# Hybrid decoder layer on one core: gate tables by one fp32r product a token, with the norm, y and routing edits that come with it

## The reference, cut to what matters

```
def peer_ffn(x, w_q, sub_keys, u_tab, v_tab):      # K = 16, 8 heads, 128 keys a side
    s = einsum('nhpd,pkd->nhpk', qry, sub_keys)
    s_top, i_top = top_k(s, K)
    cand = s_top[:, :, 0, :, None] + s_top[:, :, 1, None, :]      # 16 x 16 sums
    best, pos = top_k(cand.reshape(N, H, K * K), K)
    expert = take_along_axis(cand_id, pos)          # i * 128 + j
    gate = softmax(best)
    hid = gelu(einsum('cd,chkd->chk', xc, u_tab[expert]))
    return einsum('chk,chkd->cd', gate * hid, v_tab[expert])
```

## Time and profile before

| | us |
|---|---|
| median of 3 runs (lowest, highest) | 1108.76 (1108.48, 1110.25) |
| profiled execution | 1108.59 |
| its span in the trace | 1106.6 |
| PE busy | 1083.8 (98%) |
| DVE busy | 775.9 (70%) |
| ACT busy | 556.8 (50%) |
| POOL busy | 174.1 (16%) |

### The profile page before, as it was taken

How to read it: one execution, slowest core, us unless ns; L and a number is a source line. 1 busy time by engine, 2 the same in 40 slices (tenths; PEclk the granted TensorE clock), 3 DMA queues, 4 the chain that set the end, 5 groups by cost and what they waited for, 6 DMA issues and landing times.

```text
span 1106.6 us, 19897 instructions
## 1 busy us (share of the span) xinstructions
PE 1083.8 (98%) x6760; PEld 969.9 (88%) x6760; DVE 775.9 (70%) x1399; ACT 556.8 (50%) x903; POOL 174.1 (16%) x112
## 2 busy tenths in 40 slices
PE   9999999999999999999999999999999999999995
PEld 6888887678999999999999999998888888888884
DVE  4457657477999888898997777765555555555556
ACT  4347534554345555554455555554555444555442
POOL 2040002203000022222222545520000000000002
PEclk9999999999999999999999999999999999999998
DMA  7554444344455544445444444446555555555552
GB/s 283 186 191 153 135 170 134 107 160 132 155 171 177 177 164 166 153 157 166 152 134 159 144 139 146 133 152 228 190 192 193 197 195 190 190 194 193 197 194 96
DMA packets 52616, 186.50 MB, mean 169 GB/s; under 512 B 6224, under 2 KB 6608, under 8 KB 52576
## 3 DMA queue, kind: packets, MB, share of 16 engines
q1 hardware_dynamic: 51152, 181.82, 49.1%
q0 software_dynamic: 848, 3.15, 0.7%
q10 hardware_dynamic: 576, 1.05, 0.3%
HBM read 184.94 MB, written 1.05 MB: 168 GB/s over the span
## 4 chain that ended last, share of the span: by engine, by line
PE 73%; issue 12%; DVE 5%; POOL 5%; DMA 3%; ACT 2%; SPq 0%; DVEq 0%; POOLq 0%
PE ps L1179 12%; PE ps L1181 12%; PE ps L1180 12%; PE ps L1501 10%; PE ps L1503 10%; PE ps L1502 10%; POOL hot_j L435 5%; PE ps L1461 3%; DVE wlo L707 2%; DMA raw<-w_tiles_in 1%; ACT whi L458 1%; PE ps L1230 1%; DMA raw<-w_tiles_v 1%; PE ps L1427 1%; DMA raw<-w_tiles_u 1%
## 5 line engine op out<-in xcount | busy, mean ns | idle before, releaser
L707 DVE TENSOR_TENSOR wlo<-raw,whi 128x1024 fp32r<-128x1024 f32 x341 | 422.0, 1238 | 261.9 <-ACT whi L458 259.8
L458 ACT ACTIVATE whi<-raw 128x1024 fp32r<-128x1024 f32 x343 | 363.4, 1060 | 311.9 <-DMA raw<-w_tiles_v 170.8
L1179 PE MATMUL ps<-ahi,whi 128*128 128x256 f32 x1152 | 332.7, 289 | 1.4 <-DVE wlo L707 1.0
L1181 PE MATMUL ps<-ahi,wlo 128*128 128x256 f32 x1152 | 325.8, 283 | 0.0
L1180 PE MATMUL ps<-alo,whi 128*128 128x256 f32 x1152 | 325.7, 283 | 0.0
L1179 PEld LDWEIGHTS ps<-ahi,whi 128*128 128x128 f32 x1152 | 220.6, 191 | 1.8 <-DVE wlo L707 1.2
L1180 PEld LDWEIGHTS ps<-alo,whi 128*128 128x128 f32 x1152 | 220.8, 192 | 0.0
L1181 PEld LDWEIGHTS ps<-ahi,wlo 128*128 128x128 f32 x1152 | 220.5, 191 | 0.0
L1501 PE MATMUL ps<-whi,hhi 128*128 128x512 f32 x512 | 199.4, 390 | 0.9 <-DVE wlo L707 0.9
L1502 PE MATMUL ps<-wlo,hhi 128*128 128x512 f32 x512 | 199.2, 389 | 0.0
L1503 PE MATMUL ps<-whi,hlo 128*128 128x512 f32 x512 | 199.2, 389 | 0.0
(11 more groups left out here) (205 smaller groups left out, 910.9 us busy)
## 6 DMA issues: line engine op xcount, KB each, us to landing
raw<-w_tiles_u SPq DMA_DIRECT2D x128, 512.0 KB, 3.2
raw<-w_tiles_v SPq DMA_DIRECT2D x128, 512.0 KB, 3.3
raw<-w_tiles_in SPq DMA_DIRECT2D x63, 512.0 KB, 3.3
raw<-w_tiles_q SPq DMA_DIRECT2D x16, 512.0 KB, 3.3
raw<-w_tiles_out SPq DMA_DIRECT2D x8, 512.0 KB, 3.2
xraw<-xT ACTq DMA_DIRECT2D x4, 256.0 KB, 6.5
xt<-x POOLq DMA_DIRECT2D x1, 1024.0 KB, 6.0
out<-xt SPq DMA_DIRECT2D x4, 256.0 KB, 2.1
```

The costliest lines, as they stand in the source:

```text
L458: act.activation(whi[:, tile.slot, :], raw[:, tile.slot, :], ACT.Copy)\
L707: dve.tensor_tensor(wlo[:, tile.slot, :], raw[:, tile.slot, :], whi[:, tile.slot, :].bitcast(F32), ALU.subtract)\
L1179: pe.matmul(out, ah, bh, start=start, stop=False)
L1181: return pe.matmul(out, al, bh, start=False, stop=stop)
```

## The change

Gate tables: DVE makes only the one-hot of j (512 elements, bf16), ACT widens it. POOL makes, for each token, two 128-element vectors: (iota == i) times the high half of the gate, and the same with the low half, 8 instructions a chunk. PE does one fp32r product of 256 columns a token, into two banks a chunk (ring of two bank pairs). ACT copies the low table out of PSUM (`take_low`), DVE adds high and low (two instructions) and multiplies. The slow stretch has 28 chunks from U tile 32, the fast one 36 chunks at U tiles 88 to 123.

```
-RING = (0, 1)
+RING = (0, 4)
-HALF_CHUNKS = CHUNKS // NT
-ONE_PER_TWO, ONE_PER_TILE = 28, 92
+SLOW_CHUNKS = 28
+ONE_PER_TWO, ONE_PER_TILE = 32, 88
-SEL_AT = (23, 83)
-EXP_AT = (20, 79)
+SEL_AT = (27, 87)
+EXP_AT = (24, 83)
# POOL
-        def scale_j(c):
-            pool.wait_ge(S["hot_ready"], c + 1)
+        def scale_i(c):
             if c >= HOTS:
                 pool.wait_ge(S["g_done"], c + 1 - HOTS)
-            pool.tensor_tensor(hot_j[...], raw_ij[:, c % HOTS, 1, :, :]..., gateT[...]..., ALU.mult)
+            for k in range(BLK):
+                token = slice(c * BLK + k, c * BLK + k + 1)
+                for part, gate in enumerate((gate_hi, gate_lo)):
+                    pool.tensor_scalar(hot_g[:, c % HOTS, k, part, :], iota[:, :], sel_i[:, token],
+                                       gate[:, token].bitcast(F32), ALU.is_equal, ALU.mult)
# ACT, after the Gelu of the chunk's U tile
+        def take_low(c):
+            act.wait_ge(S["g_done"], c + 1)
+            if c > 0:
+                act.wait_ge(S["g_used"], c)
+            act.activation(g_low[:, :, :], tables(c, 1), ACT.Copy)
# DVE
         def hots(c):
-            dve.tensor_tensor(raw_ij[...], iota4 to [P, 2, P, BLK], selT to [P, 2, P, BLK], ALU.is_equal)
+            dve.tensor_tensor(raw_j[...], iota4, sel_j to [P, P, BLK], ALU.is_equal)
         def into_h(c):
-            dve.wait_ge(S["g_done"], c + 1)
-            dve.tensor_copy(H[:, there:NK, toks], g[:, there:NK, :])
-            dve.tensor_tensor(H[:, 0:there, toks], H[:, 0:there, toks], g[:, 0:there, :], ALU.mult)
+            dve.wait_ge(S["g_low_ready"], c + 1)
+            own.step(dve.tensor_tensor(low[:, 0:there, :], high[:, 0:there, :], low[:, 0:there, :], ALU.add))
+            own.step(dve.tensor_tensor(H[:, there:NK, toks], high[:, there:NK, :], low[:, there:NK, :], ALU.add))
+            own.wait()
+            dve.tensor_tensor(H[:, 0:there, toks], H[:, 0:there, toks], low[:, 0:there, :], ALU.mult)
# PE
-                last = pe.matmul(ps[:, RING[b], k * P:(k + 1) * P], hot_j[:, b, k, :], hot_i[:, b, k, :])
+                last = pe.matmul(ps[:, bank, base:base + 2 * NK], hot_j[:, b, k, :], hot_g[:, b, k, :, :])
```

```
-        for t in range(NT):
+        for m in range(T_END - TAIL, T_END):
+            values_ready(Tile(m))
+            for half in range(2):
+                last = values(Tile(m), 0, False, m == T_END - 1, (half,))
+        for half in range(2):
             for m in range(T_END - TAIL, T_END):
-                last = values(Tile(m), t, False, m == T_END - 1)
+                last = values(Tile(m), 1, False, m == T_END - 1, (half,))
```

More of the change, by code:

```diff
@@ L43 @@
 PH, NK, TOPK = 8, 128, 16
+PAIR_ROWS = ((0, 1, 16), (1, 3, 8), (3, 16, 4))
+PAIRS = sum((end - first) * width for first, end, width in PAIR_ROWS)
 ALPHA = 2.0 ** 0.25
@@ L286, in layer, with tables @@
     ps = nc.alloc_psum_tensor("ps", [P, 8, CW], F32)
-    HID = (2, 3, 4, 5)
+    HID = (6, 7, 2, 3)
+    def tables(c, part):
+        both = ps[:, RING[c % 2]:RING[c % 2] + 2, :].rearrange("p b (n a i) -> p (b n) a i", a=2, i=NK)
+        return both[:, :, part, :]
     Y_BANKS = (4, 5, 2, 3)
@@ L335, in _ @@
                     load(Tile(first + k, i, NS), src[bass.ds(i * NS + k, 1), :, :].rearrange("a p n -> p (a n)"))
[L336 to L340, removed]
+        for half in range(2):
+            cols = slice(half * CW, (half + 1) * CW)
+            sp.wait_ge(S["out_ready"], half + 1)
+            sp.dma_start(out[P:2 * P, cols], xt[:, 1, cols]).then_inc(S["stored"], 16)
         sp.wait_ge(S["stored"], 32 * NT)
@@ L686, in _, with value_tiles @@
             split_hi(Tile(T_V + k + AHEAD))
[L687 to L691, removed]
+        def value_tiles(first, end):
+            with act.Fori(first, end) as i:
+                for k in range(4):
+                    tile = Tile(T_V + k, i, 4).plus(AHEAD)
+                    split_h(tile)
+                    split_hi(tile)
+        value_tiles(1, LN2_COPIES)
+        act.wait_ge(S["in_ln2"], 128)
+        for n, b in enumerate((g2b, b2b)):
+            for half in range(2):
+                act.activation(ps[:, LN2_BANKS[n] + half, :], b[:, half * CW:(half + 1) * CW], ACT.Copy)\
+                    .then_inc(S["g2_ready"], 1)
+                value_tiles(LN2_COPIES + 2 * n + half, LN2_COPIES + 2 * n + half + 1)
+        value_tiles(LN2_COPIES + 4, TILES_V // 4 - 1)
         for m in range(T_END - 4 + AHEAD, T_END):
@@ L697, in _ @@
         ln_sqrt(1, 1)
+        for half in range(2):
+            cols = slice(half * CW, (half + 1) * CW)
+            act.wait_ge(S["out_ready0"], half + 1)
+            act.dma_start(out[0:P, cols], xt[:, 0, cols]).then_inc(S["stored"], 16)
     @block.vector
@@ L802, in y_low, with y, times_norm @@
                               ALU.subtract).then_inc(S["act_split_lo"], 1)
[L804 to L810, removed]
+        def y(b):
+            cols = slice(b * GDV, (b + 1) * GDV)
+            for t in range(NT):
+                z = proj[:, t, AT["r_a"]:AT["r_a"] + D][:, cols]
+                own.step(dve.tensor_tensor(z, z, proj[:, t, AT["gate_a"]:AT["gate_a"] + D][:, cols], ALU.mult))
+            own.wait()
+            for t in range(NT):
+                yb = proj[:, t, cols]
+                dve.tensor_tensor(yb, yb, proj[:, t, AT["r_a"]:AT["r_a"] + D][:, cols], ALU.add)\
+                    .then_inc(S["y_ready"], 1)
+        def times_norm(t, heads):
+            for h in heads:
+                f = proj[:, t, AT["r_a"] + h * GDV:AT["r_a"] + (h + 1) * GDV]
+                own.step(dve.scalar_tensor_tensor(out=f, in0=gla_banks(t, h),
+                                                  scalar=rrms[:, t * GH + h:t * GH + h + 1], in1=f,
+                                                  op0=ALU.mult, op1=ALU.mult))
+            own.wait()
         for m in range(4 * LOOPED, T_OUT):
@@ L878, in _ @@
                     dve.wait_ge(S["gates_p"], t + 1)
[L879 to L885, removed]
+                    times_norm(t, range(GH) if t == 0 else range(GH // 2))
+            if m == GLA_RMS[1]:
                 dve.wait_ge(S["gates_p"], 2 * NT)
                 dve.wait_ge(S["gate_a_ready"], 1)
-                for t in range(NT):
-                    y(t, 0)
-            if m == T_OUT - 1:
+                y(0)
+            if m == Y_TURN - 1:
                 y_low(0)
             split_lo(Tile(m + AHEAD))
+            if m == GLA_RMS[1]:
+                times_norm(1, range(GH // 2, GH))
+            if m == Y_TURN - 1:
+                y(1)
             if c == LOOPED + 1 or c == LOOPED and q == 3:
@@ L898, in _ @@
                     .then_inc(S["evac_dve"], 1)
-        for t in range(NT):
-            dve.wait_ge(S["gate_a_ready"], t + 2)
-            y(t, 1)
         y_low(1)
+        dve.wait_ge(S["gate_a_ready"], 1 + NT)
+        y(2)
+        y(3)
         for k in range(TILES_OUT - AHEAD):
             split_lo(Tile(T_OUT + k + AHEAD))
-            if k == Y_LATE - 1:
+            if k == Y_LATE:
                 y_low(2)
                 y_low(3)
[L908 to L946, removed]
@@ L948, in first_norm, with norm @@
-        def first_norm():
+        def norm(n, banks, gain, bank_done, gain_ready, tiles, done):
             def total(t, half):
                 xs = xt[:, t, half * CW:(half + 1) * CW]
-                own.do(dve.scalar_tensor_tensor(out=xs, in0=xs, scalar=ALPHA, in1=ps[:, OUTB[2 * t + half], :],
+                own.do(dve.scalar_tensor_tensor(out=xs, in0=xs, scalar=ALPHA, in1=ps[:, banks[2 * t + half], :],
                                                 op0=ALU.mult, op1=ALU.add))
@@ L1028, in routing @@
                     own.step(dve_idx(ids[:, a, 8:16], top[:, a, 8:16], s[a]))
-                own.do(dve.tensor_tensor(cand[:, :, :], top[:, 0, :, None].to_broadcast([P, TOPK, TOPK]),
-                                         top[:, 1, None, :].to_broadcast([P, TOPK, TOPK]), ALU.add))
+                at_pair = 0
+                for first, end, width in PAIR_ROWS:
+                    rows = end - first
+                    pairs = cand[:, at_pair:at_pair + rows * width].rearrange("p (a b) -> p a b", b=width)
+                    own.step(dve.tensor_tensor(pairs, top[:, 0, first:end, None].to_broadcast([P, rows, width]),
+                                               top[:, 1, None, 0:width].to_broadcast([P, rows, width]), ALU.add))
+                    at_pair += rows * width
+                own.wait()
                 yield
@@ L1152, in _ @@
                     gates(t)
+            for t in range(NT):
+                if u == SEL_AT[t]:
+                    take_sel(t)
             if u >= H_DONE:
@@ L1181, in three, with project @@
             return pe.matmul(out, al, bh, start=False, stop=stop)
-        def project(tile, c2, q):
+        def project(tile, c2, q, halves=range(NT)):
             tile_ready(tile)
-            for t in range(NT):
+            for t in halves:
```

(27 more changed lines are left out.)

218 lines of the change are left out of this document (125 added, 93 removed).

## The result

| | before | after |
|---|---|---|
| median of five runs (lowest to highest), us | 1108.76 (1108.48 to 1110.25) | 1305.51 (1304.36 to 1306.43) |
| span in the trace, us | 1106.6 | 1302.6 |
| PE / DVE / ACT / POOL busy, us | 1083.8 / 775.9 / 556.8 / 174.1 | 1132.9 / 821.5 / 595.5 / 583.6 |

The ratio is 1.1766, 95% interval 1.1753 to 1.1779: 197 us slower, outside the range. It is rival A in kind, at ten times its loss (1128 was 19 us over the kernel before). The first three rows are groups of the page: POOL's new line, both forms, and the product; the idle time before it stands behind the second bar.

A forecast was written before the change was run, and what follows sets the result against it. PE was taken as the bound, DVE close behind in the slow stretch. 1108.6 - 26.2 - 3.0 - 1.8 - 1.0 - 0.9 - 3.0 = 1072.7 for PE alone, + 5.6 fast + 1.4 slow = 1080 us; range 1071 to 1132.

The forecast's parts named there:

- rival A: POOL becomes the bound and the kernel slower: 0.40 us an instruction, 1128 us in total; chance 0.30.
- I take 0.28, the nearest row: Price of one new POOL instruction alone, from another instruction with one input of 128 fp32 elements: 0.28 us.
- the 0.75 that I gave as the upper end: Upper bound for one POOL instruction's price: half of a contended pair of POOL instructions, 1.51 / 2 us.
- 400 d: Added total if each POOL instruction is d us over 0.28: 8d a fast chunk, about 4d a slow one.
- Taking turns: Fast tile: POOL and DVE's two-input instructions alternate, together 3.6 us, 0.24 over the 3.36 period; +5.6 us in total.
- DVE's additions: DVE's two table additions cost what copy and multiplication cost, 0.25 and 0.58 us; fast tile 3.2 us for 3.36.
- PE's terms: Gate products on PE: 0.12 us a token, 0.48 a chunk instead of 0.89, fast period 3.36; 26.2 us saved.
- late-stage edits: Savings at the end 3.0 us, before the output projection 1.8, at the start of the V tiles 0.9.
- the waits beside the routing: PE's waits for POOL's `hot_j`, 3.0 us, and one for `wlo` in the first half's routing, 1.0 us, go.
- The end: From PE's last matmul to the span's end: 7.9 us instead of 10.95, by the first norm's list; 3.0 saved.
- The wait before the output projection: PE's 1.8 us wait for `alo` goes, as the first y quarter is turned inside the last input tile.
- The three waits for `hot_j`: PE's waits for POOL, 3.0 us together, go because POOL's new vectors need only the selection, made long before.

The follow-up runs named there:

- The forms: Kernel before plus a row of POOL instruction forms on spare memory beside the V tiles; 1110.1 us in one run, against 1109.35 without them.
- the run without POOL's load: Changed kernel with POOL making one of a chunk's eight vectors: 1099.43 us, and 1077.16 us with the low table's four tokens side by side in SBUF.
- packed: Changed kernel, low table's four tokens of an i side by side in SBUF: 1289.59 us with eight POOL vectors, 1116.60 with four, 1077.16 with one.
- The rest of the change without the tables: Changed kernel with the gate tables of before; schedule, late-stage edits and routing's 84 sums stay: 1100.38 us, ratio 0.992.
- the run with 256 sums: Changed kernel with the gate tables of before and also the routing's 256 sums of before instead of 84: 1105.34 us, ratio 0.9965.

## Why the prediction was wrong

**The step that failed** is "I take 0.28, the nearest row". The new instruction costs 0.775 us from start to start, 0.5 more, and above the 0.75 that I gave as the upper end. Rows 11 showed a selection by position and not a comparison with a number; the same opcode word (TENSOR_SCALAR) in front made it look near. The forms show where the 0.787 goes: compare-and-multiply costs 0.345 more than multiply-and-add, the two scalars 0.145. By my own 400 d the total would be 1080 + 200 = 1280. The other 25 us are some 0.4 us a chunk in both stretches: the formula gives 6.3 + 4 x 0.5 = 8.3 for a slow chunk and 3.6 + 8 x 0.5 = 7.6 for a fast one, measured 8.7 and 8.0. For the slow stretch it comes this near by luck. I let POOL cost only through DVE there, and POOL was the bound itself: 6.2 us alone, 8.7 with its standing, against PE's 6.24.

**Taking turns** was wrong too. I let POOL in after each two-input instruction of DVE, by rows 11. Where DVE had such instructions in a row, POOL stood through all of them (2.47 us above), 2.1 us a chunk on average (8.3 - 6.2), 2.5 in a slow one and 1.8 in a fast one. The Trainium skill, "SBUF — State Buffer", section "Who interferes with whom", says that a DVE instruction with two inputs in SBUF contends with a GpSimd instruction that reads SBUF, and of DVE's two-port modes that whoever issues first has the shared pair of ports for the whole instruction while the other blocks. The traces agree and show such blocking for two-input instructions in both directions (POOL 2.47 us instead of 0.79, the merge 2.00 instead of 0.3). They show besides that POOL can stand through several in a row. DVE's additions, which read one input from PSUM, did not hold it: beside them POOL took 0.80 (645.81).

**DVE's additions** at "what copy and multiplication cost" failed by the step in SBUF: 0.83 and 0.82 us instead of 0.54 for 360 elements, 22 us in the run without POOL's load. With all of POOL's load the same step cost 16 us. The number of elements had been right. The term was 2.9 - 0.27 + 0.6 = 3.2 for a fast tile; the tile shown takes 3.67, the last ones 4.0, and packed they fit in 3.36.

**Rival A** had the place and the sign. Its price of 0.40 was too low because it came from a two-input product (0.397 measured for 128 elements, so the row was read rightly), and the form used costs twice that. The Trainium skill, "GPSIMD Engine Reference", section 7, has about 102 cycles for a small read; for two scalars that is an estimated 0.17 us, and they measured 0.145, but this was not the main cost.

**What held.** PE's terms: 0.12 us a token, 0.48 a chunk, period 3.36; 1077.2 us with one POOL vector a chunk, where I had 1072.7 for PE alone. The rest of the change without the tables: 1099 forecast, 1100.4 measured. Here the total was met better than its parts: I had 3.0 + 1.8 + 0.9 = 5.7 us for the late-stage edits and 3.0 + 1.0 = 4.0 for the waits beside the routing, and the runs have 3.5 (with the schedule) and 5.0. The end, from PE's last matmul (1293.44, ending 1293.83) to the end of the span, takes 8.8 us, forecast 7.9, 10.95 before: the list of the first norm repeats (POOL ends 5.09 us after the last bank's addition starts, 5.16 in rows 13), but that addition starts 0.37 us after PE, behind the bank before it, and the store takes 3.3 instead of 2.7. The wait before the output projection fell from 1.8 to 0.3 and the one at the start of the V tiles from 0.9 to 0.4, where I had nothing left of it.

```profile
1293.44 0.39 PE L1562 MATMUL ps<-whi,hlo 128*128 128x512 f32 x1
...
1294.20 0.67 DVE L968 SCALAR_TENSOR_TENSOR xt<-xt,ps 128x512 f32<-128x512 f32 x1
...
1296.81 2.48 POOL L408 TENSOR_TENSOR xt<-xt,b2b 128x512 f32<-128x512 f32 x2
```

The three waits for `hot_j` I had put down to the tables' new inputs; the run with 256 sums shows that the lighter routing alone removes them (3.1 us with 256 sums, 0.2 with 84, and the old tables in both).

## What to carry to other kernels

Price a moved operation by its own form on the engine that takes it, and where no row has it, count it times its repetitions before anything else: eight unknown instructions a chunk with 3.4 us for all of them was the whole question, and a range of prices of a factor four needed a range of times as wide. Work for POOL beside a DVE full of two-input instructions has to fit into the time that DVE leaves, not into the period; here, packed, DVE took 1.5 us of a fast chunk from POOL, whether POOL had four instructions or eight. A view that turns a table for a reader belongs on the engine with time to spare (here ACT's write, +0.5 us hidden) and not on the bound.

## What the runs showed of the hardware that was not expected

- POOL's compare-and-multiply of 128 elements: 0.787 us, multiply-and-add with the same scalars 0.442, a single multiplication by one scalar 0.600 (more than that form with two steps), a copy 0.289.
- DVE reads fp32 from SBUF in steps of 512 bytes at about 2.0 ns an element ((0.83 - 0.42) / (360 - 152)) and packed at 1.1 ((0.54 - 0.30) / (368 - 144)); the same steps on the PSUM operand cost nothing extra in rows 6 ((0.58 - 0.25) / (420 - 92) = 1.0 ns). ACT writing in steps of 16 bytes took 1127 ns for 512 elements instead of 598.
- With PE idle 3 to 4.5 us before most of the fast chunks' products, the granted clock averaged 0.82 from 660 to 965 us. This is a mean of its two levels: behind the last such wait matmuls of 256 columns start 0.21 us apart at a granted clock of 0.50 (1.2 GHz, first row), and 0.12 apart at 1.00 (2.4 GHz, second row). It cost nothing that the chain shows, as PE was waiting for POOL anyway.

```profile
932.60:934.40 1.80, 1.80 (x10) 1.80 (x10) 1.13 (x2) 1.55 (x2) 0.00 (x0) 0.50 0.00 0
936.00:938.00 2.00, 2.00 (x19) 2.00 (x18) 1.38 (x3) 1.33 (x2) 0.00 (x0) 1.00 0.21 63
```
